# Decoder step with top-2 experts: seven experts' rows gathered and summed during the last expert, the last expert's rows brought to tokens by a matrix product

## The reference

```python
def moe_swiglu(h, w_router, b_router, w1, w3, w2):
    logits = (h @ w_router).astype(jnp.float32) + b_router.astype(jnp.float32)
    top_v, top_i = lax.top_k(logits, TOP_K)
    gates = jax.nn.softmax(top_v, axis=-1)
    dense_gate = jnp.sum(jax.nn.one_hot(top_i, N_EXPERTS, dtype=jnp.float32) * gates[..., None], axis=-2)
    out = jnp.zeros(h.shape, jnp.float32)
    for e in range(N_EXPERTS):
        y = swiglu(h, w1[e], w3[e], w2[e]).astype(jnp.float32)
        out = out + dense_gate[..., e:e + 1] * y
    return out.astype(h.dtype)
...
            f = moe_swiglu(hf, router_w[i], router_b[i], moe_w1[i], moe_w3[i], moe_w2[i])
        x = x + (gt * rms_norm(f, g_post_ffn[layer])).astype(x.dtype)
```

## Time and profile before

| | |
|---|---|
| runs | 1748.3, 1749.13, 1750.29 us |
| the profiled execution | 1752.45 us, span 1750.7 us |
| mean granted TensorE clock | 0.943 |
| PE busy | 1598.4 us (91%) |
| DVE busy | 1246.5 us (71%) |
| ACT busy | 981.6 us (56%) |
| POOL busy | 138.2 us (8%) |
| chain that ended last | PE 78%, DVE 10%, DMA 4%, POOL 3%, issue 2%, ACT 2% |

### The profile page before, as it was taken

The page is one execution under the profiler, slowest core; times in us unless marked ns, Lnnn a source line. Parts: engine busy times, 40 slices in busy tenths (PEclk is TensorE's granted clock), DMA queues, the critical chain, the costliest instruction groups (busy, mean ns, idle before and its releaser), DMA issues.

```text
span 1750.7 us, 22939 instructions
## 1 busy us (share of the span) xinstructions
PE 1598.4 (91%) x8712; PEld 1304.7 (75%) x8712; DVE 1246.5 (71%) x1092; ACT 981.6 (56%) x881; POOL 138.2 (8%) x130
## 2 busy tenths in 40 slices
PE   5869999889899769879999999999999999999991
PEld 2449999688785547558888888888888888888881
DVE  2455544377783642368888888888888888889884
ACT  1134443243332432357787777777777777777771
POOL 0000000014541331100000000000000000000001
PEclk9679999989999969679999999999999999999996
DMA  9965555765468325769999999999999999999972
GB/s 322 375 219 168 172 172 175 246 225 180 155 217 287 133 72 193 263 245 369 380 375 383 369 383 382 366 391 379 367 388 368 378 375 372 387 375 370 389 277 88
DMA packets 249295, 513.45 MB, mean 293 GB/s; under 512 B 9977, under 2 KB 69545, under 8 KB 249217
## 3 DMA queue, kind: packets, MB, share of 16 engines
q1 hardware_dynamic: 243691, 492.49, 78.5%
q0 software_dynamic: 4768, 17.37, 2.6%
q10 hardware_dynamic: 766, 2.65, 0.4%
HBM read 498.58 MB, written 14.35 MB: 293 GB/s over the span
## 4 chain that ended last, share of the span: by engine, by line
PE 78%; DVE 10%; DMA 4%; POOL 3%; issue 2%; ACT 2%; SPq 0%; POOLq 0%; DVEq 0%; ACTq 0%
PE wide L477 22%; PE wide L478 22%; PE wide L479 22%; POOL phase L1799 2%; DVE phase L1498 2%; PE wide L910 1%; PE wide L537 1%; PE wide L526 1%; DVE w_lo L1727 1%; POOL phase L1805 1%; DMA ring<-in_ada_ffn_w 1%; DVE w_lo L393 1%; DMA ring<-in_cache_v 1%; DMA ring<-in_ada_mix_w 1%; ACT w_hi L1225 1%
## 5 line engine op out<-in xcount | busy, mean ns | idle before, releaser
L1727 DVE TENSOR_TENSOR w_lo<-ring,w_hi 128x2048 fp32r<-128x2048 f32 x336 | 768.1, 2290 | 116.2 <-ACT w_hi L1225 115.0
L1225 ACT ACTIVATE w_hi<-ring 128x2048 fp32r<-128x2048 f32 x336 | 643.3, 1919 | 212.4 <-PE wide L479 212.3
L477 PE MATMUL wide<-w_hi,xe_hi 128*128 128x512 f32 x896 | 355.5, 397 | 7.8 <-DVE xe_lo L1732 6.0
L479 PE MATMUL wide<-w_hi,xe_lo 128*128 128x512 f32 x896 | 349.9, 391 | 0.0
L478 PE MATMUL wide<-w_lo,xe_hi 128*128 128x512 f32 x896 | 349.5, 390 | 0.0
L477 PE MATMUL wide<-tHi,w_hi 128*128 128x264 f32 x672 | 198.4, 295 | 28.1 <-DVE mLo L1416 28.1
L393 DVE TENSOR_TENSOR w_lo<-ring,w_hi 128x2048 fp32r<-128x2048 f32 (+1 forms) x58 | 138.9, 2399 | 109.4 <-ACT w_hi L974 108.9
L478 PE MATMUL wide<-mLo,w_hi 128*128 128x264 f32 x736 | 212.4, 289 | 0.0
L477 PEld LDWEIGHTS wide<-w_hi,xe_hi 128*128 128x128 f32 x896 | 168.6, 188 | 45.8 <-issue 6.4
L479 PEld LDWEIGHTS wide<-w_hi,xe_lo 128*128 128x128 f32 x896 | 168.6, 188 | 36.0
L478 PEld LDWEIGHTS wide<-w_lo,xe_hi 128*128 128x128 f32 x896 | 168.9, 188 | 33.4
(11 more groups left out here) (276 smaller groups left out, 1708.4 us busy)
## 6 DMA issues: line engine op xcount, KB each, us to landing
ring<-in_moe_w SPq DMA_DIRECT2D x336, 1024.0 KB, 7.2
ring<-in_ffn_w SPq DMA_DIRECT2D x30, 1024.0 KB, 5.3
ring<-in_ada_mix_w SPq DMA_DIRECT2D x24, 1024.0 KB, 7.8
ring<-in_ada_ffn_w SPq DMA_DIRECT2D x24, 1024.0 KB, 14.3
ring<-in_w_q SPq DMA_DIRECT2D x12, 1024.0 KB, 8.8
ring<-in_cache_k SPq DMA_DIRECT2D x24, 512.0 KB, 4.9
ring<-in_cache_v SPq DMA_DIRECT2D x24, 512.0 KB, 6.5
ring<-in_w_kv SPq DMA_DIRECT2D x8, 1024.0 KB, 6.7
```

The lines of the kernel that those rows point to most:

```text
L477: pe.matmul(out, a[0], b[0], start=start, stop=False, skip_group_check=True)
L479: return pe.matmul(out, a[1], b[0], start=False, stop=stop, skip_group_check=True)
L1225: act.activation(w_hi[:, (NSPLIT + k) % PAIRS, :], ring[:, slot, :], ACT.Copy).then_inc(hi_done, 1)
L1727: dve.tensor_tensor(w_lo[:, i, :], ring[:, slot, :], w_hi[:, i, :].bitcast(F32), ALU.subtract).then_inc(lo_done, 1)
```

## The change

The last expert's rows no longer go through DRAM, and the other seven experts' rows are fetched while the last one runs.

- A selection matrix `pick` (tokens by the last expert's 128 rows) holds a token's gate where the token's rank is the row's number, and zero elsewhere. TensorE makes the row numbers with one product (`ones` by `before`), VectorE compares and multiplies (three instructions), TensorE turns the three tiles, ScalarE copies them to `pickT`. All this is before the first expert.
- GpSimd's `collect_early` runs after the store of expert 6. For each tile it clears two buffers in `hT`, and fetches with two indirect DMAs the rows whose number is under 7 x 128; what belongs to expert 7 stays zero. One pair of buffers serves all three tiles.
- VectorE's `early_sum` makes the gated sum of a tile into `part`, ahead of its slabs 14, 20 and 26 of the last expert.
- At the end the last `ye` isn't stored. TensorE multiplies `pickT` with it (six fp32 matmuls of 512 columns into the free PSUM banks), VectorE adds that to `part`.
- VectorE's reading of the flag and its branch now stand behind these additions. ScalarE takes a first root of a constant ahead of the tiles, and does square and root of a tile one behind the other.

```diff
+            pe.wait_ge(ht_taken, KC)
+            pe.matmul(bank[2][:, 0:P], ones, before, start=True, stop=True).then_inc(count_row, 1)
             pe.wait_ge(gate_rows, 1)
...
             mm.then_inc(gate_spread, 1)
+            pe.wait_ge(pick_ready, 1)
+            for q, n in enumerate(rows):
+                mm = pe.transpose(bank[2][:, P * (q + 1):P * (q + 1) + n], pick[0:n, q, :], ident[0:n, 0:n])
+            mm.then_inc(pick_turned, 1)
             pe.wait_ge(gate_taken, 1)
...
             experts(0)
+            pe.wait_ge(pick_taken, 1)
+            pe.wait_ge(y0_copied, NE + 1)
+            pe.wait_ge(y1_copied, NE + 1)
+            for q, n in enumerate(rows):
+                for h in range(2):
+                    mm = pe.matmul(wide[q][0:n, 512 * h:512 * (h + 1)], pickT[:, P * q:P * q + n], ye[:, 512 * h:512 * (h + 1)], start=True, stop=True)
+                mm.then_inc(merged, 1)
             overflow = pe.value_load(flag[0:1, 0:1], min_val=0, max_val=1)
...
+            act.wait_ge(pick_turned, 1)
+            act.activation(pickT, bank[2][:, P:P + NT], ACT.Copy).then_inc(pick_taken, 1)
             act.sem_inc(silu_done, 1)
...
+            act.activation(tail_s[:, 0, 3:4], eps1, ACT.Sqrt)
             for q, n in enumerate((P, P, NB)):
                 act.wait_ge(f_ready, q + 1)
-                act.activation(back[0:n, q, :], fout[0:n, q, :], ACT.Square, accum_out=tail_s[0:n, q, 0:1]).then_inc(act_step, 1)
-            for q, n in enumerate((P, P, NB)):
-                act.wait_ge(act_step, steps[0] + q + 1)
+                link(act.activation(back[0:n, q, :], part[q][0:n, :], ACT.Square, accum_out=tail_s[0:n, q, 0:1]))
                 act.activation(tail_s[0:n, q, 1:2], tail_s[0:n, q, 0:1], ACT.Sqrt, bias=eps1[0:n], scale=1.0 / D).then_inc(f_std, 1)
...
             dve.wait_ge(flag_ready, 1)
+            dve.wait_ge(count_row, 1)
+            for q, n in enumerate(rows):
+                ins = dve.tensor_scalar(pick[0:n, q, :], bank[2][0:n, 0:P], r_a[0:n, q, 1, NE - 1:NE], gate[0:n, q, NE - 1:NE], ALU.is_equal, ALU.mult)
+            ins.then_inc(pick_ready, 1)
             dve.wait_ge(gate_turned, 1)
...
+            def early_sum(q):
+
+                n = rows[q]
+                dve.wait_ge(early_in, 32 * (q + 1))
+                link(dve.tensor_scalar(early[0][0:n, :], early[0][0:n, :], gpair[0:n, 0, q:q + 1], None, ALU.mult))
+                dve.scalar_tensor_tensor(part[q][0:n, :], early[1][0:n, :], gpair[0:n, 1, q:q + 1], early[0][0:n, :], ALU.mult, ALU.add)\
+                   .then_inc(early_done, 1)
...
                 for k, (m, j, half) in enumerate(eslabs):
+                    if last and c == 0 and k in (14, 20, 26):
+                        early_sum((k - 14) // 6)
...
             experts(0)
+            tiles = tuple(enumerate((P, P, NB)))
+            dve.wait_ge(early_done, 3)
+            for q, n in tiles:
+                dve.wait_ge(merged, q + 1)
+                dve.tensor_tensor(part[q][0:n, :], part[q][0:n, :], wide[q][0:n, :], ALU.add).then_inc(f_ready, 1)
             overflow = dve.value_load(flag[0:1, 0:1], min_val=0, max_val=1)
...
-            for q, n in tiles:
-                dve.wait_ge(y_back[q], 32)
-                link(dve.tensor_scalar(back[0:n, q, :], back[0:n, q, :], gpair[0:n, 0, q:q + 1], None, ALU.mult))
-                dve.scalar_tensor_tensor(fout[0:n, q, :], back[0:n, 3 + q, :], gpair[0:n, 1, q:q + 1], back[0:n, q, :], ALU.mult, ALU.add)\
-                   .then_inc(f_ready, 1)
...
+            def collect_early():
+
+                for q, n in enumerate(rows):
+                    if q:
+                        pool.wait_ge(early_done, q)
+                    pool.memset(hflat[0:n, 0:2 * D], 0.0).then_inc(early_zero, 1)
+                    pool.wait_ge(early_zero, q + 1)
+                    for i in range(2):
+                        pool.indirect_dma_start(early[i][0:n, :], None, y_rows[0][0:EARLY_ROWS, :],
+                                                bass.IndirectOffsetOnAxis(ap=row[0:n, 0, i, q:q + 1], axis=0),
+                                                bounds_check=EARLY_ROWS - 1, oob_is_err=False).then_inc(early_in, 16)
+                pool.wait_ge(early_done, 3)
...
+                    if done == NE - 1:
+                        pool.wait_ge(xe_turned, 2 * NE)
+                        collect_early()
+                        pool.wait_ge(merged, 3)
+                        pool.sem_inc(y_free, 1)
+                        continue
                     pool.wait_ge(y0_copied, done + 2)
...
-            collect(0, y_back)
```

More of the change, by code:

```diff
@@ L285, in yoco_step @@
         r_d = at(11896, 2, 3)
+        pickT = over("pickT", "ada", 0, [P, NT], F32)[:, :]
+        pick = at(11906, 3, P)
+        xflat = xT[:, :, :].rearrange("p a b -> p (a b)")
+        part = [xflat[:, 0:D], xflat[:, D:2 * D], over("part_s", "const", 0, [P, D], F32)[:, :]]
+        early = [hflat[:, 0:D], hflat[:, D:2 * D]]
         back = ring[:, 0:3, :].rearrange("p a (b n) -> p (a b) n", n=D)
@@ L336, in yoco_step @@
         y_stored, y_free, f_ready, f_std, y_done = (sem(n) for n in ("y_stored", "y_free", "f_ready", "f_std", "y_done"))
-        y_over = sem("y_over")
-        y_back = [sem(f"y_back{q}") for q in range(3)]
+        y_over, over_added = sem("y_over"), sem("over_added")
+        count_row, pick_ready, pick_turned, pick_taken = (sem(n) for n in ("count_row", "pick_ready", "pick_turned", "pick_taken"))
+        early_zero, early_in, early_done, merged = (sem(n) for n in ("early_zero", "early_in", "early_done", "merged"))
         moe_ready, flag_ready = sem("moe_ready"), sem("flag_ready")
@@ L1774, in _ @@
                     experts(c)
-            tiles = tuple(enumerate((P, P, NB)))
-            for q, n in tiles:
-                dve.wait_ge(y_back[q], 32)
-                link(dve.tensor_scalar(back[0:n, q, :], back[0:n, q, :], gpair[0:n, 0, q:q + 1], None, ALU.mult))
-                dve.scalar_tensor_tensor(fout[0:n, q, :], back[0:n, 3 + q, :], gpair[0:n, 1, q:q + 1], back[0:n, q, :], ALU.mult, ALU.add)\
-                   .then_inc(f_ready, 1)
+                dve.wait_ge(f_ready, 3)
+                dve.wait_ge(y_over, 16 * 6)
+                for i in range(2):
+                    for q, n in tiles:
+                        ins = dve.scalar_tensor_tensor(part[q][0:n, :], back[0:n, 3 * i + q, :], gpair[0:n, i, q:q + 1], part[q][0:n, :], ALU.mult, ALU.add)
+                    ins.then_inc(over_added, 1)
+                    dve.wait_ge(over_added, i + 1)
             for q, n in tiles:
@@ L1840, in scatter, with collect_over @@
                                                 htok[0:n, q, :], None, bounds_check=ROWS[over] - 1, oob_is_err=False).then_inc(scattered, 16)
-            def collect(over, done):
+            def collect_early():
[4 more added lines that the diff above has]
+                    pool.wait_ge(early_zero, q + 1)
+                    for i in range(2):
+                        pool.indirect_dma_start(early[i][0:n, :], None, y_rows[0][0:EARLY_ROWS, :],
+                                                bass.IndirectOffsetOnAxis(ap=row[0:n, 0, i, q:q + 1], axis=0),
+                                                bounds_check=EARLY_ROWS - 1, oob_is_err=False).then_inc(early_in, 16)
+                pool.wait_ge(early_done, 3)
+            def collect_over():
+                pool.memset(ring[:, 0:3, :], 0.0).then_inc(zero_ready, 1)
+                pool.wait_ge(zero_ready, 3)
                 for q, n in enumerate(rows):
                     for i in range(2):
-                        pool.indirect_dma_start(back[0:n, 3 * i + q, :], None, y_rows[over][:, :],
-                                                bass.IndirectOffsetOnAxis(ap=row[0:n, over, i, q:q + 1], axis=0),
-                                                bounds_check=ROWS[over] - 1, oob_is_err=False).then_inc(done[q], 16)
+                        pool.indirect_dma_start(back[0:n, 3 * i + q, :], None, y_rows[1][:, :],
+                                                bass.IndirectOffsetOnAxis(ap=row[0:n, 1, i, q:q + 1], axis=0),
+                                                bounds_check=ROWS[1] - 1, oob_is_err=False).then_inc(y_over, 16)
+                pool.wait_ge(y_over, 16 * 6)
             rows = (P, P, NB)
@@ L1872, in experts @@
                     pool.dma_start(slab_rows(y_rows, e, c), ye[:, :]).then_inc(y_stored, 16)
-                    pool.wait_ge(y_stored, 16 * (done + 1))
+                    pool.wait_ge(y_stored, 16 * (done + 1 - min(c, 1)))
                     pool.sem_inc(y_free, 1)
```

8 lines of the change are left out of this document (5 added, 3 removed).

## The result

The changed kernel took **1740.87 us** (median of 5 runs, 1738.07 to 1742.33) against 1749.26 for the kernel before beside it (5 runs, 1748.3 to 1750.7): a ratio of 0.9948, 95% interval 0.9936 to 0.996. A second set of runs gave 1737.78 against 1748.71, 0.9939 (0.9926 to 0.9953). So 8.4 and 10.9 us were won of 13.5 forecast. The profiled execution took 1738.07 us.

The account below looks back on a forecast made before the run. Bound: TensorE's chain to the last product at 1714.8 us, then a 36 us tail with TensorE idle. Terms -17.2 + 2.1 + 1.6 = -13.5 us gave 1735.6 against the median 1749.13, range 1732 to 1742.

Parts of the forecast that it names:

- The tail: After the last product: selection matmuls and additions replace store, wait and six gathers; 17.2 us less (14.8 to 18.2).
- the code behind VectorE's branch: Between third addition and normalising: fetching code after the branch takes 1.3 us, bounds nothing to 3.66.
- the table load: ScalarE's load for the root comes ahead of the first sum, while the matmuls run, and costs nothing.
- The three sums: Inside the last expert: each 2.1 us on VectorE delays TensorE 0.7 us, together +2.1 us (nothing to 6.3).
- Before the first expert: Building the selection matrix on the path delays the first weight subtraction by 1.6 us (1.27 to 3.0).
- The half clock: Rival: clock falls before the selection products, six matmuls take 10.4 us instead of 5.2; 1740.8 us, chance 0.08.
- The late gathers: Rival: tiles 1 and 2 in the last expert land 2.3 us late each; +4.6, 1740.2 us, chance 0.11.
- the cover: Last expert: tile 1's gather lands at 1652.5, wanted at 1657.8, so covered by 5 us; tile 2 likewise.
- The starving of POOL: Rival: indirect issues held through two VectorE subtractions, 5.6 us, make two tiles 10.9 late each; 1757.4 us, chance 0.03.

Follow-up runs that it names:

- split sums: Changed kernel with two early sums split, multiply and multiply-add at different slabs, the third whole behind the last subtraction: 1738.25 us, 0.9938.
- the last kernel: As the kernel with all parts, but multiplies ahead of slabs 14, 25, 35 and multiply-adds ahead of 17, 28, 38: 1729.18 us, 0.9876.
- the second profile of before: The kernel before the change, run and profiled once more unchanged: 1746.0 us in one run.
- the kernel with all parts: Changed kernel plus VectorE's and ScalarE's branches ahead, sums split, selection matrix behind gate rows and weight copies, tile 0 normalised before third addition: 1734.21 us, 0.9906.
- branch ahead: Changed kernel with VectorE's flag reading and branch moved ahead of its last copy, last copy and additions in both arms: 1735.78 us, 0.9931.

## Why the prediction was right, and what it had wrong

The verdict (faster), the mechanism and the range hold: 1740.87 lies within 1732 to 1742, and so does 1737.78. The forecast, 1735.6, was 5.3 and 2.2 us too low, for these reasons.

**The tail, forecast -17.2, came to -15.4** between the two first profiles (35.91 to 20.54). The step that failed is the code behind VectorE's branch, "between nothing and 3.66 us I take 1.3, the row of the same engine". It took 3.0, from 1723.0 to 1725.96. The 1.3 was the distance from the branch to two packets on the queue that brings code. That a packet is on the queue does not say that the engine can go on: in after the packets came just as early, 1.0 and 1.3 us behind the branch, and VectorE went on 1.4 us after the end of the second. TensorE's branch of 3.66 us, which I had kept as the far bound, was the nearer row. ScalarE's branch, at 1716.46, shows the same in after's chain of waits:

```profile
1716.46 0.05 ACTq L1293
1716.51 2.60 issue
1719.11 1.28 ACT L1298
```

It cost nothing there, as forecast for the table load: tile 0's root is out at 1721.97, before the third addition ends. All else in the tail came close to what was worked out: matmuls at the full clock, additions of 1.22 us, the third ending 7.57 us after the last copies began (forecast 7.36), and 10.24 from the first reciprocal to the end (10.3). The rule on instruction fetch in the Trainium skill, page "Runtime: NRT & Kernel Launch", section "Instruction fetch mechanics", by which a taken branch to code outside the fetched window waits for that code to be brought in, agrees with these rows: from a branch to the next instruction it is 2.5 to 3.0 us on ScalarE and 2.8 to 3.4 on VectorE, over the nine profiles of changed kernels.

**The three sums, forecast +2.1, came to +2.06** (112.57 to 114.63), 0.69 us for each sum (forecast 0.7), with TensorE waiting for the low part behind each of them as forecast. The split sums show the cause for two of them: it was not the work of 2.1 us, but having it in one piece ahead of one subtraction. For the third it was shown in part only, since that one was moved where nothing is left to delay; where it is split too, in the last kernel, it still costs 0.6 us, ahead of an activation block's low part.

**Before the first expert, forecast +1.6.** From the flag to the store of expert 6 it is 864.51 in before and 866.08 in after: +1.57. But only 0.64 of it lies ahead of the first product; the other 0.93 lies in the seven experts, where the change does nothing and the two profiles of before differ by 1.03. The pieces ahead of the first product are those of the forecast: the gate rows are copied 1.2 us later after the flag (1.99 in before, 3.18 in after; forecast 1.27), and the first subtraction then starts 0.64 later behind VectorE's copies, nearly all of it a wait of 0.57 for ScalarE (forecast 0.33), which has the selection matrix to copy first. Its three transposes took 0.89 us where 0.5 had been put in as an estimate. Against these 1.9 us the gate products ran 1.2 faster in after. Against the second profile of before the whole stretch is 3.1 longer, for the clock of the gate products alone moves it by 2.7. So the mechanism held, and the agreement to a tenth is luck; the averages above say about 2.

So by the traces the sum is -15.4 + 2.1 + 1.6 = -11.7 where -13.5 was forecast. The two profiled executions differ by 14.4 us in their own times (1752.45 and 1738.07), since the flag stood 2.8 us earlier in the second; the medians of that set differ by 8.4. Only one execution of each is traced, so which stage took the rest in the others stays open. The flag's time, which spreads by 6.6 us over the profiles with nothing of the change ahead of it, would be enough.

**The rivals.** The half clock at the selection products did not come in after, where they follow a pause of 0.87 us; in the kernel with all parts it came for a part of them, behind 2.28. The late gathers did not come: they landed 7.1 to 9.7 us after their issue began, and VectorE waited for none. But the cover was less than the forecast 5 us: tile 1's second gather began at 1646.64 and landed 8.3 us later, 1.6 us before VectorE wanted it at 1656.53. The starving of POOL is real, at half the price that I gave it. I had allowed for an issue held through two subtractions, 5.6 us; every issue seen got through behind the first, in 1.0 to 3.1 us, and the cover took that. The Trainium skill, page "SBUF — State Buffer", section "Who interferes with whom", has a lock that would fit these rows: a VectorE instruction with two SBUF inputs and a GpSimd one that reads SBUF keep each other out. The rows agree in so far as issues begun inside a subtraction of two SBUF inputs end 0.79 to 0.94 us after it, while those begun between two take 1.00 to 1.06. That the indirect issue reads SBUF, and so that this lock is the cause, is inferred and not shown.

## What to carry to other kernels

A taken branch can cost far more than its row, some 3 us here, not 0.06; put it where its engine waits for something else in any case, and check that nothing delays the branch out of that cover. Small work moved onto a nearly full engine should be cut to the size of that engine's lead and spread, since the lead comes back within a few slabs. Where single runs spread more than an edit is worth, cut the span at marks that the edit does not move, and compare stage by stage.

## What was not expected of the hardware

POOL's issue of an indirect DMA depends on VectorE: 1.01 us with VectorE idle, 1.5 to 3.1 when begun inside a subtraction, with the DMA share at 0.02 as at 1.04, while the subtractions kept their 2.29 us. And of three gains that were each shown alone, one undid another by moving a branch: VectorE's branch stood 4.9 us ahead of the last copy in "branch ahead", and 1.9 ahead of the last product's end here, so the copy came 1.4 us late, and the clock went down behind it.
